# A stick-breaking, RG-LRU and memory-attention layer on one core: row factors, the last weight chunk, the probabilities and the output weights take other places in the first three bodies

## What is computed

```
h = rmsnorm(x) * norm_g ;  proj = h @ w_in            # 1024 -> 3072, six groups of 512
SB  : 8 heads x 64, q and k normed, stick-breaking attention, strictly causal
      w[t,s] = sigmoid(z[t,s]) * prod over s < r < t of (1 - sigmoid(z[t,r])) ;  out = w @ v
LRU : width-4 causal convolution, gates r and i (blocks of 64), h_t = a_t h_(t-1) + sqrt(1-a_t^2) i_t x_t
XA  : 4 heads x 64, q and k normed, softmax attention into 256 memory tokens (mem @ w_mem_kv, normed)
out = x + concat(SB*silu(gate), LRU*silu(gate), XA*silu(gate)) @ w_out   # 1024 -> 1024
```

## Time and profile before

| | us |
|---|---|
| median of 3 runs (lowest to highest) | 1612.38 (1612.06 to 1615.23) |
| the profiled execution's own time | 1613.46 |
| its span | 1611.7 |
| PE busy | 1539.3 |
| DVE busy | 1066.6 |
| ACT busy | 882.9 |
| POOL busy | 315.8 |

### The profile page before, as it was taken

The page is one execution under the profiler, slowest core; times in us unless marked ns, Lnnn a source line. Parts: engine busy times, 40 slices in busy tenths (PEclk is TensorE's granted clock), DMA queues, the critical chain, the costliest instruction groups (busy, mean ns, idle before and its releaser), DMA issues.

```text
span 1611.7 us, 29935 instructions
## 1 busy us (share of the span) xinstructions
PE 1539.3 (96%) x10886; PEld 751.9 (47%) x10886; DVE 1066.6 (66%) x1932; ACT 882.9 (55%) x1593; POOL 315.8 (20%) x305
## 2 busy tenths in 40 slices
PE   4897899999999999999999999999999999999976
PEld 1343444444444444444444444444444444444432
DVE  5876767666666766666676666667666666766662
ACT  5865666544556654455565445556544555654451
POOL 2221122121222222112222211122211112221110
PEclk9998999999999999999999999999999999999997
DMA  9353454554545455454545545454454545445443
GB/s 369 138 144 76 115 125 112 127 135 104 130 111 127 108 127 134 104 137 104 127 114 124 134 101 140 103 126 119 120 132 106 135 107 123 120 117 132 111 82 104
DMA packets 368711, 201.62 MB, mean 125 GB/s; under 512 B 333792, under 2 KB 334240, under 8 KB 367520
## 3 DMA queue, kind: packets, MB, share of 16 engines
q1 hardware_dynamic: 368384, 200.98, 49.1%
q10 hardware_dynamic: 288, 0.13, 0.0%
HBM read 70.73 MB, written 50.53 MB: 75 GB/s over the span
## 4 chain that ended last, share of the span: by engine, by line
PE 69%; ACT 12%; issue 5%; DVE 1%; SPq 0%; DMA 0%; ACTq 0%; POOL 0%; POOLq 0%; DVEq 0%
PE bank L1572 21%; PE bank L1574 21%; PE bank L1573 21%; ACT fail_and_take L879 2%; PE bank L1616 2%; ACT L872 1%; ACT L895 1%; ACT spare L902 1%; ACT L913 1%; ACT L917 1%; PE bank L1713 1%; PE bank L1724 1%; ACT fail_and_take L887 1%; PE bank L1744 1%; DVE spare L1360 1%
## 5 line engine op out<-in xcount | busy, mean ns | idle before, releaser
L1572 PE MATMUL bank<-w_pair,x_hi 128*128 128x512 f16 x1536 | 587.4, 382 | 12.0 <-DVE w_pair L1060 8.7
L1574 PE MATMUL bank<-w_pair,x_lo 128*128 128x512 f16 x1536 | 586.1, 382 | 0.0
L1573 PE MATMUL bank<-w_pair,x_hi 128*128 128x512 f16 x1536 | 586.1, 382 | 0.0
L1572 PEld LDWEIGHTS bank<-w_pair,x_hi 128*128 128x128 f16 x1536 | 151.0, 98 | 189.2 <-issue 11.8
L1574 PEld LDWEIGHTS bank<-w_pair,x_lo 128*128 128x128 f16 x1536 | 151.2, 98 | 184.0 <-issue 5.0
L1573 PEld LDWEIGHTS bank<-w_pair,x_hi 128*128 128x128 f16 x1536 | 151.3, 98 | 167.6 <-issue 4.6
L951 ACT ACTIVATE spare<-xy,columns 128x1024 f16<-128x1024 f32 x32 | 36.8, 1148 | 345.5 <-DVE columns L1434 345.5
L1572 PE MATMUL bank<-wo_pair,y_hi 128*128 128x512 f16 x512 | 196.3, 383 | 8.2 <-DMA y_lo<-spare 8.2
L1573 PE MATMUL bank<-wo_pair,y_hi 128*128 128x512 f16 x512 | 196.2, 383 | 0.0
L1574 PE MATMUL bank<-wo_pair,y_lo 128*128 128x512 f16 x512 | 196.1, 383 | 0.0
L637 POOL TENSOR_TENSOR fail_and_take<-fail_and_take,seen 128x512 f32<-128x512 f32 x32 | 42.8, 1338 | 698.5 <-ACT fail_and_take L780 698.5
(11 more groups left out here) (245 smaller groups left out, 2420.1 us busy)
## 6 DMA issues: line engine op xcount, KB each, us to landing
xy<-in_x SPq DMA_DIRECT2D x32, 512.0 KB, 3.4
x_t<-in_x_turned SPq DMA_DIRECT2D x32, 512.0 KB, 4.8
spare<-in_x SPq DMA_DIRECT2D x32, 512.0 KB, 4.2
out<-spare SPq DMA_DIRECT2D x32, 512.0 KB, 2.6
gate_kept<-gate SPq DMA_DIRECT2D x32, 256.0 KB, 2.2
v_kept<-v_sb SPq DMA_DIRECT2D x32, 256.0 KB, 2.1
fail_and_take<-v_sb SPq DMA_DIRECT2D x64, 128.0 KB, 2.3
q_kept<-q_t SPq DMA_DIRECT2D x32, 256.0 KB, 4.0
```

Of the source, the lines that this page charges most:

```text
L1572: pe.matmul(dst, hi[:, k, :], pair[:, 0, k, :], start=k == 0, stop=False)
L1573: pe.matmul(dst, hi[:, k, :], pair[:, 1, k, :], start=False, stop=False)
L1574: last = pe.matmul(dst, lo[:, k, :], pair[:, 0, k, :], start=False, stop=k == KD - 1)
```

## The change

It touches only the bodies of n = 0, 1 and 2.

- **Body 0, tile 1's row factor.** The squares of tile 1 stand first on ScalarE, ahead of chunk 0's high pieces; they stood behind chunk 4's. GpSimd's factor stands behind `lru_rate`, the diagonal ahead of chunk 1's factor, its product ahead of the memory's first product, `scale_rows` ahead of the keys' sums.
- **Body 0, chunk 5.** Factor, high and low pieces follow chunk 4's at once; the norms of the heads, their high and low halves and the memory's values stand behind them. `x_hi` and `x_lo` of tile 1 stand ahead of `v`'s and the heads' halves.
- **Body 1.** PE projects first and scores then (`near_scores` stands behind `project(1)`); the keys' halo on ScalarE stands behind `out_sum(6)`; the memory's values are split ahead of the convolution. The probabilities' high half follows the exponentials, their low half the norms, and SP turns them ahead of queries and keys. The row factor on GpSimd stands between its two gate products, the diagonal ahead of the heads' low halves, its product ahead of `project(5)`. `out_sum(7)` and `out_rows_top` stand at the end of the body.
- **Body 2.** `out_wide` stands behind `project(0)`, `out_chunk_factors` behind the first head sums. The pieces of chunk 6 stand one place later (none is left in body 1), and two pieces of chunk 7 stand behind the heads' halves, where one stood.
- `out_diag` lies in the output weights' staging area instead of `y_lo`. `y_un` of tile 0 is written in body 2.

The diff, cut to its core:

```diff
@@ sync: body
+                early = isinstance(n, int) and n == 1
+                def probs_turned():
+                    have(sp, s["heads"], n - 1)
+                    have(sp, s["p_high"], n - 1)
+                    turn(turned[:, 0], halves[:, 0, :], p_turned)
+                    have(sp, s["p_low"], n - 1)
+                    turn(turned[:, 1], halves[:, 1, :], p_turned)
+                if early:
+                    probs_turned()
                 if A:                       # the turns of queries and keys
...
-                if B:                       # the five lines above stood here
+                if B and not early:
+                    probs_turned()
@@ gpsimd: body
                 if first:
                     lru_rate()
+                    row_factor()
                     memory_rows()
                     band_masks()
...
                     pool.tensor_tensor(in_g[:, :, :], in_g[:, :, :], xc[:, :, :], ALU.mult).then_inc(s["ui_done"], 1)
+                    if isinstance(n, int) and n == 1:
+                        row_factor()
@@ scalar: body
+                def row_squares():
+                    have_dma(act, x_loaded, n + 1)
+                    if not first:
+                        have(act, s["xq_sum"], n)
+                    if B:
+                        have(act, s["w_low"], n - 1)
+                    act.activation(take_waste if B else squares.bitcast(BF16), xy[:, :], ACT.Square, accum_out=ss_x[:, :]
+                                   ).then_inc(s["x_sq"], 1)
...
                 if first:
+                    row_squares()
                     chunk_high(0)
                     chunk_sum(1)
                     chunk_high(1)
                     chunk_sum(2)
...
                 if early:
                     out_sum(6)
+                    key_halo()
                 if isinstance(n, int) and n == 2:
-                    chunk_high(6, 1)
+                    chunk_high(6, 0)
...
+                if early:
+                    probs_high()
+                if X and not first:
+                    row_squares()
...
+                if A and not first:
+                    heads_high()
                 if first:
-                    for m in range(MT):
-                        memory_values(m)
                     chunk_high(5)
                 if isinstance(n, int) and n == 2:
+                    chunk_high(7, 0)
                     chunk_high(7, 1)
...
+                if first:
+                    memory_values(0)
+                    rows_high()
...
+                if first:
+                    heads_high()
+                    memory_values(1)
...
                 if early:
-                    chunk_high(6, 0)
+                    out_sum(7)
@@ vector: body
                     chunk_rows(1)
+                    row_diagonal()
                     chunk_factor(1)
...
                 if early:
+                    memory_values_split()
                     memory_keys_turned()
+                    convolution(1)
                 if third:
-                    chunk_low(6, 1)
+                    out_chunk_factors()
+                    undo_of_y(p)
+                    chunk_low(6, 0)
+                if first:
+                    scale_rows()
...
                     next_chunk(4)
+                    chunk_factor(5)
+                    silu_lru()
+                    chunk_low(5)
+                    silu_stick()
...
                 if first:
-                    row_diagonal()
+                    rows_low()
+                    values_low()
+                if early:
+                    probs_low()
...
+                if A and not first:
+                    silu_lru()
                 if early:
-                    out_rows_top()
+                    row_diagonal()
...
+                if third:
+                    chunk_low(7, 0)
+                    chunk_low(7, 1)
+                if early:
+                    scale_rows()
...
                 if early:
-                    chunk_low(6, 0)
+                    out_rows_top()
@@ tensor: body
                 project(0, [(s["gate_sb"], n - 1), (s["out0_read"], n - 3)])
...
+                early = static and n == 1
+                if early:
                     values_wide()
+                if static and n == 2:
+                    out_wide()
+                if B and not (after or early):
+                    near_scores(1)
                 project(1, [(s["v_read"], n - 1), (s["out_ready"], n - 3)])
+                if early:
                     memory_keys_turn()
                     near_scores(1)
                 if static and n == 0:
                     chunk_wide(2)
+                    spread_rows()
                     memory_product(0, 0)
...
+                if early:
+                    spread_rows()
                 project(5, [(s["gate_l"], n)])
```

More of the change, by code:

```diff
@@ L672, in body @@
                     mask(0)
[L673 to L680, removed]
+                if X and not (isinstance(n, int) and n in (0, 1)):
+                    row_factor()
                 if first:
@@ L794, in body, with key_halo @@
                     chunk_sum(2)
-                if B and not after:
+                early = isinstance(n, int) and n == 1
+                def key_halo():
                     have(act, qk_turned, n - 1, 96)
@@ L799, in body, with probs_high @@
                     last.then_inc(s["k_halo"], 1)
[L800 to L803, removed]
+                def probs_high():
+                    have(act, s["p_done"], n - 1)
+                    have_turned(act, w_turned, n - 1)
+                    act.activation(halves[:, 0, :], probs[:, :, :].rearrange("p h m -> p (h m)"), ACT.Copy, scale=WTOP
+                                   ).then_inc(s["p_high"], 1)
+                if B and not (after or early):
+                    key_halo()
                 if A:
@@ L920, in body @@
                     chunk_high(7, 2)
-                if B:
-                    have(act, s["p_done"], n - 1)
-                    have_turned(act, w_turned, n - 1)
-                    act.activation(halves[:, 0, :], probs[:, :, :].rearrange("p h m -> p (h m)"), ACT.Copy, scale=WTOP
-                                   ).then_inc(s["p_high"], 1)
+                if first:
+                    memory_values(0)
+                    rows_high()
+                if B and not early:
+                    probs_high()
                 if isinstance(n, int) and n == 2:
@@ L940, in body @@
                     weights_high(0)
-                if X:
-                    have(act, s["x_scaled"], n + 1)
-                    if A:
-                        have(act, proj_done[5], n)
-                    act.activation(x_hi[:, :, :], x_t32[:, :, :], ACT.Copy).then_inc(s["x_hi_done"], 1)
+                if first:
+                    heads_high()
+                    memory_values(1)
+                if X and not first:
+                    rows_high()
                 if B:
@@ L1202, in convolution @@
                         last.then_inc(s["conv"], 1)
-                if B and not after:
-                    convolution(1)
                 if early:
                     memory_values_bound()
+                elif B and not after:
+                    convolution(1)
                 def head_sums(signal, done, at, heads):
@@ L1362, in body @@
                     last.then_inc(s["h_done"], 1)
-                if X and not first:
+                if X and not (first or early):
                     row_diagonal()
@@ L1371, in body @@
                                              ALU.mult, ALU.mult).then_inc(s["gx_done"], 1)
-                    have(dve, s["p_high"], n - 1)
-                    dve.scalar_tensor_tensor(halves[:, 1, :], probs[:, :, :].rearrange("p h m -> p (h m)"), WTOP,
-                                             halves[:, 0, :], ALU.mult, ALU.subtract).then_inc(s["p_low"], 1)
+                    if not early:
+                        probs_low()
                 if third:
@@ L1619, in near_scores, with spread_rows @@
                     last.then_inc(s["scores"], 1)
+                def spread_rows():
+                    have(pe, s["x_diag"], n + 1)
+                    if B:
+                        have(pe, s["gates_read"], n - 1)
+                    pe.matmul(SMALL[:, 0:P], ones[:, :], diagonal_of(n + 1), start=True, stop=True).then_inc(s["x_wide"], 1)
                 def out_first():
@@ L1748, in body @@
                     near_scores(0)
+                if early:
+                    spread_rows()
                 project(5, [(s["gate_l"], n)])
-                if X and not (static and n == 0):
+                if X and not (static and n in (0, 1)):
                     spread_rows()
```

133 lines of the change are left out of this document (62 added, 71 removed).

## The result

The changed kernel took 1634.32 us (median of 4 runs, 1633.18 to 1636.17) against 1612.68 for the kernel before: a ratio of 1.0132, 95% interval 1.0115 to 1.015. It is slower by 21.6 us; I had forecast 1630.3, in a range of 1625.5 to 1633.5, so the direction and the stall are there, and 4 us more, which lies outside the range. Timed again beside the experiments it took 1635.18 (ratio 1.0136, 1.0121 to 1.0152).

The account below looks back on a forecast made before the run. PE, busy 96% of the span, was taken to bound the kernel. A stall of 18.9 less 1.0 given back made +17.9: 1613.46 became 1631.4, and 1630.3 us as median (profiled run 1.08 above median); range 1625.5 to 1633.5.

Parts of the forecast that it names:

- the stall: First body: ScalarE's squares wait for the second tile's rows until 39.0 us, so chunk 0 starts 18.9 us later.
- lead: PE's gain on the old trace, stall taken off: 6.9, 10.6, 5.0, then 1.9 us at the third body's spread product.
- rival 1: First body: the second tile's rows land before ScalarE is free, no stall, 1611.4 us; chance 5%.
- the give-back: The three bodies' other edits regain 1.9 or 0.2 us; 1.0 taken, bounds 5.0 and −1.5.
- The wait that I had put ahead of the second body's fifth product: Second body: PE idles 4 us because VectorE waits for the probabilities' high half; fifth product at 122.1 us.
- the 6.80 us of the values' product: Second body: PE's 6.80 us wait for turned probabilities ahead of the values' product goes away.
- The two pieces of chunk 7 ahead of the square root: Third body: two pieces stand where one of 1.14 us stood, taking 1.14 + 1.9 us off the lead.
- the half clock: Second and third body: PE may run at 1.2 GHz after idling, losing 1.6 to 1.7 us per stretch.
- rival 3: Second and third body: new PE waits bring three half-clocked stretches and out_wide stays late, 1632.8 us; chance 13%.

Follow-up runs that it names:

- E1: Changed kernel with the second tile's rows loaded right behind the first weight chunk: 1614.19 us, ratio 1.001 to the kernel before.
- E6: E1 with two third-body orders changed: last chunks' factor ahead of the convolution, chunk 7's second piece behind the gate's sigmoid: 1612.8 us, ratio 1.0004.
- E7: E6 with VectorE's third-body scan and row diagonal ahead of the gate's SiLU and chunk 7's second piece: 1608.15 us, ratio 0.9966.
- E8: E1 plus 20 matmuls nobody reads on PE ahead of the third body's spread product: 1612.9 us, ratio 1.0001.
- E3: Kernel before with only the second tile's squares moved ahead of chunk 0 on ScalarE: 1630.12 us, ratio 1.0112.
- E9: E8 plus 18 more such matmuls on PE ahead of the second body's spread product: 1613.05 us, ratio 1.0003.

## Why the prediction was right in kind and 4 us short

All landmarks below are means of four profiles of each kernel; "lead" is 18.56 less the difference.

| landmark of PE | before | changed | difference | lead | lead forecast |
|---|---|---|---|---|---|
| first product | 22.77 | 41.33 | 18.56 | 0 | (18.9 as the stall) |
| second tile's first product | 91.58 | 103.46 | 11.88 | 6.7 | 6.9 |
| third tile's first product | 141.01 | 150.85 | 9.84 | 8.7 | 10.6 |
| third body's fifth product | 175.07 | 191.01 | 15.94 | 2.6 | 5.0 |
| spread product, third body | 184.12 | 203.17 | 19.05 | −0.5 | 1.9 |
| loop's first product | 195.76 | 217.37 | 21.62 | −3.1 | 1.0 taken |

**The stall was right.** The squares are ScalarE's first instruction of the body, at 38.5 us and not 39.0, and the first product is 18.56 us late against the 18.9 forecast. The load came in its order, 28.2 us after its issue; rival 1, the early landing, didn't happen, but E1 shows what it would have been worth.

**The step that failed is the give-back.** I took +1.0 us, and the runs show −3.1: this term is 4.1 us off. The stall gave 0.3 of it back, and the kernel before took 1612.68 beside the result where I had 1612.38, which leaves the 4.0. By its own steps:

- The changed kernel's landmarks were nearly right up to the spread product. With the stall taken off, the means are 84.90, 132.29, 172.45 and 184.61, where I had 84.95, 132.0, 171.8 and 183.9. The wait that I had put ahead of the second body's fifth product came ahead of the spread product, which the change puts before it (4.50 us); the 6.80 us of the values' product went. `out_wide()` stands 10.0 us behind the third tile's first product in all four, where I had 10.2; PE stood 3.01 of them ahead of it and not 5, because its product ahead of it ran at a granted clock of 0.57 over the first 4 us.
- The kernel before was read wrongly. I subtracted from 142.6, 176.76 and 185.81; the means of four profiles are 141.01, 175.07 and 184.12. One execution's rows were taken as exact, and every lead from the second body on was counted 1.6 to 1.7 us too large.
- The two pieces of chunk 7 ahead of the square root took the share that I gave them. ScalarE in the first trace:

```profile
190.22 1.14 ACT L773 ACTIVATE wo_pair<-wo_pair,columns 128x1024 f16<-128x1024 f32 x1
193.32 1.15 ACT L773 ACTIVATE wo_pair<-wo_pair,columns 128x1024 f16<-128x1024 f32 x1 [1.96 <-issue]
...
195.78 0.42 ACT L958 ACTIVATE rec_g<-rec_g 128x256 f32<-128x256 f32 x1
```

What I had missed is that VectorE's scan then stands behind chunk 7's pieces as well, although its inputs are there (E6): taking it out of that queue was worth 4.65 us of medians (E7). It is a gain that I hadn't seen, and no part of the miss: the spread product itself came 0.7 us behind its forecast.

- From the spread product to the loop's first product the kernel before takes 11.64 us in each of its four profiles. The changed one takes 14.67, 13.09, 14.51 and 14.52, 2.56 more on average. That is the half clock behind 5.13 us of idling (6.81 in the second), and with the idling filled E8 takes 11.64 too. I had put 0 to 1.7 us on it, from a stretch behind 2.09 us of idling, and half of that into the sum. The place of this term was right and its size was not; rival 3, which had named the mechanism, stood at 1632.8 and 13%. How much of the 2.56 us the other edits cost and how much comes with the stall isn't shown: E3, with the stall alone and 2.01 us of idling, takes 13.33 us in its one profile, and E1, without the stall, 14.39.

In sum: 1.9 by the landmarks, less 1.7 for the rows of before, 0.7 for the changed kernel's own path and 2.6 for the half clock (I had 0.9 for it), is −3.1.

One sum of the prediction is wrong, though nothing hangs on it: PE's idle time in the three stages of the earlier trace rows is 12.9 + 11.1 + 4.1 = 28.1 us, not 29.9.

The Trainium skill ("TensorE: Matmul & The Clock Gate", Part 1) says that the number of slow matmuls at a kernel's start differs from run to run of one kernel and shouldn't be fitted to a count. The four profiles show the same in the middle of the kernel: behind the same 5.13 us (6.81 in one) PE lost 1.5 to 3.0 us. So the price should have been a range as wide as that, and the range of the forecast should have reached further up than 1633.5.

The medians say 21.6 to 22.5 us, the four profiles 21.8. E1 (20.1 to 21.0 below the changed kernel) and E3 (17.6 above the one before) lie on either side of the stall's 18.56. Their intervals, 3 to 5 us wide, allow it. The one profile of E1 puts the loop's first product at 199.15, 3.4 us behind the mean of before, and that of E3 puts it at 216.57, 20.8 us behind. By E1 the other edits cost 1.7 us, by the changed kernel less E3 4.2 to 5.1; the landmarks' 3.1 lies between, and I leave it at that.

## What to carry to other kernels

Before a step is put at the head of an in-order queue, look up when its data land, not only whether its engine is idle: a 1 us step in a 2.9 us gap cost 18.6 us because its load stood behind 11 MB of others, and one earlier issue undid that. When a lead is carried through several waits, follow each instruction that the last wait hangs on through every queue in which it stands; here three orders, none of them on PE, decided between 1614 and 1608 us. And price PE's idling with the clock behind it, from more than one profile, since that part differs by 1 to 3 us between executions of one kernel.

## What the runs showed of the hardware

- The same idle time of PE can be followed by a different stretch in each execution. Behind the 2.51 us ahead of the second tile's first product the granted clock over the 4 us from 104.5 us on was 1.00, 0.57, 0.74 and 0.64 in the four profiles of the changed kernel. Behind the 1.99 us ahead of its third tile's first product it was 0.57 over 4 us in all four. Behind the 2.02 us ahead of the spread product in the kernel before it was 1.00 over 6 us in all four, and behind 2.01 us at the same place in E3 it was 0.72. Keeping PE at work for 4.48 us with matmuls that nobody reads went with a clock of 1.00 behind it in E8's profile; where 2.49 us of idling were left behind them, it was 0.72 over 6 us (E9).
- The load of 512 KB took 28.2 us behind four weight chunks, the memory, its weights and the gate blocks, and 7.9 us behind one chunk; from 22 to 41 us the transfers ran at 370 GB/s.
- Executions of the kernel before spread from 1609.9 to 1615.7 us, and its profiles show where: 3.0 us ahead of the loop, 3.1 behind it, and the loop's own 1349 us in between (1348.9 to 1349.3 us from its first product to the end of a wait of 7.25 us in the last bodies, in all the traces of all kernels).
